# A hybrid decoder step on eight cores: the recurrence's scan writes into another buffer, and every engine's order of work is chosen with new offsets

## The reference, cut to what matters

```python
u = rmsnorm(x, norm_g)
lx, lg, sb, scg, sh, sg, q, qg, mg = jnp.split(u @ w_in, SPLIT_POINTS, axis=-1)
# A: conv(4) -> RG-LRU, SiLU gate path
xc, new_lru_buf = causal_dwconv(lx, lru_buf, lru_conv_w); xc = xc + lru_conv_b
#   r, i = sigmoid(xc @ wa + ba), sigmoid(xc @ wx + bx)      (block diagonal, 6 blocks of 128)
#   log_a = -8 * r * softplus(-lam);  a = exp(log_a)
#   b = sqrt(1 - exp(2*log_a)) * (i * xc);   h_t = a_t * h_(t-1) + b_t
hs, new_h = rglru(xc, lru_h, ...);   z_a = (hs * silu(lg)) @ lru_wo
# B: z_b = (silu(sg) * sb * conv3(scg * sh)) @ sconv_wo
# C: z_c = (softmax(q k' / sqrt(128)) v * silu(qg)) @ xa_wo   (4 heads, 256 memory tokens)
g_a, g_b, g_c = jnp.split(sigmoid(mg), 3, axis=-1)
y = x + (g_a * z_a + g_b * z_b + g_c * z_c) @ w_out          (then a final rmsnorm)
```

## Time and profile before

| | us |
|---|---|
| median of 3 runs (742.28 to 742.45) | 742.34 |
| the profiled execution's own time | 742.75 |
| its span on the slowest core (first to last instruction) | 741.4 |
| spans of the other cores | 738.9 to 740.6 |
| TensorE busy | 704.7 (95%) |
| VectorE busy | 400.1 (54%) |
| ScalarE busy | 345.5 (47%) |
| GpSimd busy | 203.9 (27%) |

### The profile page before, as it was taken

How to read it: one execution, slowest core, us unless ns; L and a number is a source line. 1 busy time by engine, 2 the same in 40 slices (tenths; PEclk the granted TensorE clock), 3 DMA queues, 4 the chain that set the end, 5 groups by cost and what they waited for, 6 DMA issues and landing times.

```text
span 741.4 us, 12905 instructions; the slowest of 8 cores (738.9 to 741.4 us)
## 1 busy us (share of the span) xinstructions
PE 704.7 (95%) x4745; PEld 449.8 (61%) x4745; DVE 400.1 (54%) x391; ACT 345.5 (47%) x457; POOL 203.9 (27%) x268
## 2 busy tenths in 40 slices
PE   1899999999999999999999999999999999999995
PEld 0566666656566566566666666666666666665442
DVE  2455236856459469549784889731323122124666
ACT  3565468585696696894932221212121221213444
POOL 4554001002004002001041436351636363422000
PEclk9999999999999999999999999999999999999998
DMA  8994931112212321222142687853392926038834
GB/s 177 254 242 110 154 67 29 30 30 44 29 29 29 44 29 29 29 34 33 23 82 38 118 172 186 145 80 35 57 138 37 140 35 93 1 118 237 289 147 169
DMA packets 29485, 69.74 MB, mean 94 GB/s; under 512 B 3456, under 2 KB 7872, under 8 KB 29168
## 3 DMA queue, kind: packets, MB, share of 16 engines
q0 software_dynamic: 18000, 31.60, 30.1%
q1 hardware_dynamic: 11424, 37.32, 15.5%
HBM read 90.73 MB, written 9.88 MB: 136 GB/s over the span
## 4 chain that ended last, share of the span: by engine, by line
PE 86%; ACT 4%; DMA 4%; DVE 3%; issue 2%; POOL 0%; SPq 0%; DVEq 0%; ACTq 0%; POOLq 0%
PE PP L649 68%; PE PP L1228 7%; PE PP L692 6%; DMA R<-xp 2%; PE PP L993 2%; ACT R L845 1%; DMA R<-R 1%; PE PP L739 1%; PE PP L923 1%; DMA R<-ck 1%; DVE R L1067 1%; PE PP L985 1%; DVE R L1070 0%; ACT R L727 0%; ACT R L849 0%
## 5 line engine op out<-in xcount | busy, mean ns | idle before, releaser
L649 PE MATMUL PP<-R 128*128 128x344 bf16 x3768 | 558.6, 309 | 7.4 <-ACT R L845 4.3
L649 PEld LDWEIGHTS PP<-R 128*128 128x128 bf16 x3768 | 366.2, 98 | 198.3 <-issue 18.0
L1164 ACT ACTIVATE R<-PP 128x688 f32<-128x688 f32 x72 | 53.5, 743 | 209.5 <-PE PP L649 197.3
L1173 DVE SCALAR_TENSOR_TENSOR R<-R,PP 128x688 f32<-128x688 f32 x72 | 62.1, 868 | 133.1 <-PE PP L649 125.1
L136 POOL DMA_DIRECT2D R<-w_in x68 | 37.6, 553 | 272.1 <-PE PP L649 237.6
L692 PE MATMUL PP<-R 128*128 128x344 bf16 x336 | 53.7, 317 | 3.8 <-DVE R L742 3.2
L1228 PE MATMUL PP<-R 128*128 128x512 bf16 x256 | 55.7, 379 | 0.0
L1177 POOL TENSOR_TENSOR R<-R 128x688 f32<-128x688 f32 x24 | 41.1, 1723 | 45.3 <-DVE R L1173 36.5
L1182 POOL TENSOR_TENSOR R<-R 128x688 bf16<-128x688 f32 x24 | 40.8, 1722 | 20.9 <-DVE R L1173 20.7
L832 DVE SCALAR_TENSOR_TENSOR R<-R 128x2048 f32<-128x2048 f32 x18 | 42.3, 2349 | 7.3 <-ACT R L829 6.2
L692 PEld LDWEIGHTS PP<-R 128*128 128x128 bf16 x336 | 32.8, 100 | 20.2 <-issue 4.4
(11 more groups left out here) (137 smaller groups left out, 572.2 us busy)
## 6 DMA issues: line engine op xcount, KB each, us to landing
R<-w_in POOLq DMA_DIRECT2D x68, 256.0 KB, 4.6
R<-xp SPq DMA_DIRECT2D x32, 512.0 KB, 10.0
R<-ck SPq DMA_DIRECT2D x16, 512.0 KB, 5.1
y_p<-R SPq DMA_DIRECT2D x15, 512.0 KB, 2.6
R<-cv POOLq DMA_DIRECT2D x16, 256.0 KB, 7.8
R<-w_out POOLq DMA_DIRECT2D x8, 256.0 KB, 7.8
R<-xa_wo POOLq DMA_DIRECT2D x14, 128.0 KB, 4.9
R<-lru_wo POOLq DMA_DIRECT2D x8, 192.0 KB, 4.0
```

The costliest lines, as they stand in the source:

```text
L649: return lambda e: e.matmul(ps.ap[:, b * 512:b * 512 + BLK], lhs(k), rhs[:, k, c:c + BLK], start=(k == 0), stop=(k == nk - 1))
L1164: G.act(lambda e, ps=pg[u], th_=th_: e.activation(out=b3(th_.ap), in_=pv(ps), func=AF.Tanh, scale=0.5), UW, [pg[u].tok], [th_.tok], Px - E ...
L1173: G.dve(lambda e, zp=zp, th_=th_, dst=dst: e.scalar_tensor_tensor(out=b3(dst.ap), in0=b3(th_.ap), scalar=1.0, in1=pv(zp), op0=ALU.add, op1 ...
```

## The change: what it does

Four parts.

1. **Scan.** L861, L863, L865 write `a2` in place of `xc`, and L867, L869, L870 read `a2`. The token of `a2` is one for the whole buffer, where `xc` had one for the prompt columns and one for the sample columns. Nothing is added or removed.
2. **Offsets.** Each task gets a key of step and engine (`x2.sp`, `gates3.pe`, `final16.dve`), and a table adds an offset to its priority.
3. **Planner's numbers.** A unit's matmul 0.1465 to 0.1457, a final tile 3.46 to 3.45, the DMA rate at the start 155e3 to 150e3.
4. **Tags** that name the steps.

The table has one entry for nearly every step and engine; of it the lines that the prediction speaks of are shown.

```diff
+SHIFT = {
+    ".dve": -39.5, ".sp": 2.5, "first0.pool": -192.5, "first1.pool": 7, "first2.pool": -16, "x0.sp": -139, "x0.pool": -40.5,
+    "x0.dve": -42, "x0.pe": -6.5, "first3.pool": 11, "x1.sp": -137, "x1.act": 47.5, "x1.pool": -54, "x1.pe": -84.5, "x1.dve": -8,
+    "first4.pool": 47.5, "x2.sp": -349, "x2.act": -2.5, "x2.pool": -7, "x2.dve": 69, "x2.pe": 10.5, "first5.pool": 50, "x3.sp": -107,
+    "x3.pe": -16, "x3.dve": -42.5, "first6.pool": 24, "x4.sp": -40, "x4.act": 0.5, "x4.pool": -15.5, "x4.dve": 2.5, "x4.pe": -60,
+    "first7.pool": 3.5, "x5.sp": -30, "x5.act": 66.5, "x5.pool": -143.5, "x5.pe": 12, "x5.dve": -123, "first8.pool": 8.5, "x6.sp": -29.5,
...
+    "B_sb0.pe": 18.5, "B_sb0.dve": 20, "gates1.pe": 2, "gates1.act": -6, "rec1.act": 31, "rec1.pool": -30, "attend0.pool": 60,
...
+    "A_lx2.act": -2, "conv2.act": -38.5, "conv2.dve": -10.5, "B_sb1.pool": 2, "B_sb1.pe": 2, "B_sb1.dve": 79, "gates2.pe": 2.5,
...
+    "gates3.pe": 11.5, "gates3.act": -31, "rec3.act": -13.5, "rec3.dve": -10.5, "rec3.pool": -6, "attend2.pool": -488, "attend2.pe": -6,
...
+    "conv4.pool": 15.5, "B_sb3.pool": 7.5, "B_sb3.pe": -39, "B_sb3.dve": 0.5, "gates4.pe": -13.5, "gates4.act": 30.5, "rec4.act": -20,
...
+    "sconv5.sp": -56, "scores.sp": -4, "scores.dve": 51.5, "scores.act": -102, "scores.pe": 41.5, "merge00.pe": -41.5, "merge00.act": 7,
...
+    "final14.dve": -23.5, "final14.act": -39, "final15.sp": 53.5, "final15.pe": 108, "final15.dve": 28, "final15.act": 119.5,
+    "final16.sp": 162, "final16.pe": 107.5, "final16.dve": 68.5, "final16.act": 17,
+}
...
+        t.key = f"{self.tag}.{eng}"
+        t.prio += SHIFT.get(t.key, 0.0)
...
-                rate = 155e3 if start < 58.0 else 280e3
+                rate = 150e3 if start < 58.0 else 280e3
...
-            G.pe([mm(k, b) for k in range(nk) for b in range(2)], nk * 2 * 0.1465, reads, [ps.tok], prio, hold)
+            G.pe([mm(k, b) for k in range(nk) for b in range(2)], nk * 2 * 0.1457, reads, [ps.tok], prio, hold)
...
-            G.dve(lambda e: e.tensor_tensor_scan(out=xc[:, 0:T], data0=thr[:, 0:T], data1=thi[:, 0:T], initial=0.0,
-                                                 op0=ALU.mult, op1=ALU.add), T, t_thr + t_thi, [t_xcP], P, mode=0.5)
-            G.dve(lambda e: e.tensor_tensor(out=xc[:, T:TT], in0=thr[:, T:TT], in1=SIT[:, n * 6 + 3, :], op=ALU.mult), TS,
-                  [t_thr[2], m_SIT.t], [t_xcS], P)
...
-            G.dve(lambda e: e.tensor_tensor(out=gA[:, n, :], in0=xc, in1=gA[:, n, :], op=ALU.mult), TT,
-                  [t_xcP, t_xcS] + t_gA[n], t_gA[n], P)
...
+            G.dve(lambda e: e.tensor_tensor_scan(out=a2[:, 0:T], data0=thr[:, 0:T], data1=thi[:, 0:T], initial=0.0,
+                                                 op0=ALU.mult, op1=ALU.add), T, t_thr + t_thi, [m_a2.t], P, mode=0.5)
+            G.dve(lambda e: e.tensor_tensor(out=a2[:, T:TT], in0=thr[:, T:TT], in1=SIT[:, n * 6 + 3, :], op=ALU.mult), TS,
+                  [t_thr[2], m_SIT.t], [m_a2.t], P)
+            G.dve(lambda e: e.tensor_tensor(out=a2[:, T:TT], in0=a2[:, T:TT], in1=thi[:, T:TT], op=ALU.add), TS,
+                  [t_thi[2], m_a2.t], [m_a2.t], P)
+            G.dve(lambda e: e.tensor_tensor(out=gA[:, n, :], in0=a2, in1=gA[:, n, :], op=ALU.mult), TT,
+                  [m_a2.t] + t_gA[n], t_gA[n], P)
+            G.pool(lambda e: e.tensor_copy(SO[:, n, 3:4], a2[:, T - 1:T]), 0.2, [m_a2.t], [t_SO], P + 5)
+            G.pool(lambda e: e.tensor_copy(SO[:, n, 22:38], a2[:, T:TT]), 0.2, [m_a2.t], [t_SO], P + 5)
```

More of the change, by code:

```diff
@@ L212 @@
 class Task:
-    __slots__ = ("i", "eng", "dur", "fns", "reads", "writes", "prio", "hs", "tset", "npred", "succ", "pf", "dma", "preds", "start", "gate", "etset", "xgate", "stores")
+    __slots__ = ("i", "eng", "dur", "fns", "reads", "writes", "prio", "hs", "tset", "npred", "succ", "pf", "dma", "preds", "start", "gate", "etset", "xgate", "stores", "key")
+SHIFT = {
[47 rows of a table added]
+    "sconv5.sp": -56, "scores.sp": -4, "scores.dve": 51.5, "scores.act": -102, "scores.pe": 41.5, "merge00.pe": -41.5, "merge00.act": 7,
[24 rows of a table added]
+}
 EXP = frozenset((0, 6))
@@ L229, in __init__ @@
         self.touch = {}
+        self.tag = ""
     def _shared(self, k):
@@ L724, in p0 @@
         def p0(ti, src, nr, dst, gcols, tdst, prio, wait):
+            G.tag = f"x{ti}"
             x_, xn_, ps = Handle(xring), Handle(xnring), Handle(PS, 1)
@@ L752, in build_program @@
             while len(w_toks) < len(first) and len(w_toks) < i + LEAD:
+                G.tag = f"first{len(w_toks)}"
                 hw, lhs = wload(w_in_cols(first[len(w_toks)]), -200 + i)
@@ L764, in build_program @@
             p0(17 + i, memp[i * 128:(i + 1) * 128, :], 128, mnT[:, :, i * 128:(i + 1) * 128], pT[:, 8:16], t_mn[i], -80 + i, w_toks[-1:])
+        G.tag = "states"
         for k in ("sin", "out"):
@@ L827, in branch_A_lx @@
                 G.act(lambda e, p=p: e.copy(out=p.dst(lxp, 3), in_=p.src()), p.n, [p.tok], [t_lx[p.u]], P - EV + p.u, psum=True)
+            G.tag = f"conv{n}"
             cw = lambda k: pT[:, 16 + k * 6 + n:17 + k * 6 + n]
@@ L848, in branch_A_gates @@
             P = P - 4 - AB
+            G.tag = f"rec{n}"
             G.act(lambda e: e.activation(out=a2, in_=thr, func=AF.Exp, scale=dv[:, 6 + n:7 + n], bias=dv[:, 6 + n:7 + n]), TT,
@@ L887, in branch_B_c @@
             P += 7.02
+            G.tag = f"sh{n}"
             for u, ps in enumerate(proj(C_SH + n * 128, P)):
@@ L890, in branch_B_c @@
                       [ps.tok, t_sc[u]], [t_ci[u]], P - EV + u)
+            G.tag = f"sconv{n}"
             sw = lambda k: pT[:, 64 + k * 6 + n:65 + k * 6 + n]
@@ L962, in heads_q @@
             P += 8
+            G.tag = "qs"
             tq = m_tq.ap.rearrange("p (c b h) -> p c b h", c=2, h=4)
@@ L980, in attend @@
                 P1 = P + tb * 8.55
+                G.tag = f"att{hd}{tb}"
                 ps, ps2, pe_, rd_ = Handle(PS), Handle(PS), Handle(pering), Handle(rdring)
@@ L1011, in step @@
             nonlocal pos
+            G.tag = f.__name__.replace("branch_", "") + str(a[0])
             f(*a, pos)
@@ L1019, in build_program @@
         step(branch_A_lx, 0)
+        G.tag = "kv"
         kv(pos + KVP)
@@ L1025, in build_program @@
             if n < NCH:
+                G.tag = f"gates{n}"
                 branch_A_gates(n, pos + 10.73)
@@ L1151, in build_program @@
             if j == 0:
+                G.tag = "scores"
                 sample_scores(P, 8.0)
             if j == 4:
+                G.tag = "values"
                 sample_values(P - 5, 2.5)
@@ L1158, in build_program @@
                 Px = P + xi * 12
+                G.tag = f"merge{j}{x}"
                 ths = [Handle(thring) for _ in range(NU)]
@@ L1185, in build_program @@
             if j == NJS:
+                G.tag = "fix"
                 fix_samples(P + 6)
@@ L1237, in whole_tile @@
             tile_in(ti, x_)
-            G.pe([f for b in range(2) for f in tile_mm(ti, b, lambda b=b: ps.ap[:, b * 512:(b + 1) * 512])], 3.46,
+            G.pe([f for b in range(2) for f in tile_mm(ti, b, lambda b=b: ps.ap[:, b * 512:(b + 1) * 512])], 3.45,
                  tile_reads(ti * 128, ti * 128 + 128), [ps.tok], P)
@@ L1312, in build_program @@
             P = PF + i * 3.5
+            G.tag = f"final{i}"
             if ti == 16:
```

4 lines of the change are left out of this document (removed), and 60 rows, old and new, of the table SHIFT.

## The result

The changed kernel takes 747.35 us (median of 4 runs, 746.13 to 749.7) against 742.31 (742.17 to 742.45): ratio 1.007, 95% interval 1.0049 to 1.0091. It is slower by 0.7%, and 2.9 us above the top of the range.

What follows compares the result with a forecast made beforehand. TensorE bounds the kernel, busy 704.7 of 741.4 us, leaving 36.7 idle. Start -0.6, gates -2.7, scan 0, merge 0, end -0.7 and new waits +1.0 make -3.0: 739.3 on the median, own range 736.5 to 741.5, full range 734.5 to 744.5.

Steps and rivals of the forecast that it cites:

- New waits: Anywhere in the new order: one misfit between estimated and real durations, +1.0 us, ends 0 and +5.0.
- the score copy: Merge: VectorE waits 8.76 us for the 32 KB copy, priced by the planner at 3.2; TensorE lost 1.4.
- Start: Before the first projections: late `par` costs +0.5, tile 5 is 1.0 us earlier; -0.6 in all, ends -3.0 and +1.0.
- Gates and front: TensorE's waits for ScalarE to empty PSUM, 5.4 us: half removed, -2.7, ends -5.4 and +1.0.
- Scan: Six scans: earlier free `xc` saves only ScalarE time that TensorE's work hides; 0, ends -0.8 and +0.3.
- Merge: VectorE's wait before L1076 for the score copy comes later; 0, ends -1.4 and +5.0.
- End: Behind the last matmul: L1250 goes first and the last store has 256 KB; -0.7 us, ends -1.1 and +0.5.
- the gates' waits under 3 us: Sign for the front: TensorE's waits for L845 under 3 us in all, against 4.3.
- the second block's wait under 1 us: Sign for the start: the wait before 33.31, for tile 5's L742, falls from 1.75 to under 1 us.
- The first piece at 21.3 to 21.7: Sign for the start: first projection piece at that time after three L742 back to back, against 21.04 before.
- a busy time of TensorE within 1 us: Sign for the whole kernel: busy time, 704.7 us before, stays the same; a larger move means wrong reasons.
- The third rival: Merge, score copy uncovered: +5.0 us, giving 744.3, or 746.5 if the clock falls too; chance 0.16.

Runs made afterwards that it cites:

- run 1: Changed kernel with one weight load of the fourth block's branch A put ahead of the six small GpSimd copies: 741.39 us, ratio 0.9986 to the kernel before.
- run 2: Changed kernel with that weight load ahead of the copies and two merge weight loads ahead of GpSimd's waiting sums: 737.50 us, ratio 0.9933 to the kernel before.
- run 7: Kernel before with one front weight load, issued 60 us ahead of its use, put behind the load near 239 us: 749.72 us, ratio 1.0097.
- run 10: Changed kernel with three loads earlier, three products ahead of the last tiles' transposes, and the start in the old order: 734.55 us, ratio 0.9898 to before.
- run 5: Kernel before, its order kept, with only the scan's edit (scan in `a2`, L863's small product moved behind L861): 742.49 us, ratio 1.0002.
- run 4: Changed kernel with the three weight loads earlier and `par` with its small operations first: 739.69 us, ratio 0.9959 to the kernel before.
- run 11: Changed kernel, same offsets, planner's price of GpSimd's six small copies raised from 0.2 to 2.3 us, planned anew: 760.22 us, ratio 1.0248 to the kernel before.
- run 8: Kernel before with one front weight load made late and eight small GpSimd fills ahead of it: 751.06 us, ratio 1.0115.
- run 3: Changed kernel with the parameter DMA `par` first on SP and the small operations on it first, weight loads untouched: 746.73 us, ratio 1.0065 to before.

## Why the prediction was wrong

**The failed step is "New waits", taken as +1.0 with an upper end of +5.0.** On the slowest core of the profiled execution it was 9.0 of waits for weights and 4.5 of clock behind two of them, 13.5; at the median, 2.35 lower, some 11 (an estimate from these two times). The step argued from the one misfit it had seen, the score copy, and asked of no other producer how early it is. The DMAs that GpSimd issues were priced nowhere in the sum but at the start, though the change moves nearly all of them. The trace of before held the warning: copies of 2.2 us beside equal ones of 0.2, right ahead of a weight load. Runs 1, 2 and 7 show the mechanism, by removal and by making it.

**The metric was left out too.** The forecast was made for one core. The waits differ by core (2.4 to 9.0 us of `w_in`), and the time is the worst of eight. Core 4 ended at 734.7, 6.7 under the slowest core before; core 1 at 748.3. The average core, at most 1.1 us above before, missed the forecast of -3.0 by 3 to 4; the rest of the miss, which is 8.0 by the medians, is the spread between cores, for which the sum had no term.

**The sum without the new waits came out near, and in part by luck.** It was -4.0. With the late loads removed (run 2) the kernel is 5.0 us under before by the ratio. But the front gained almost three times its forecast, and losses for which no term stood took the difference away.

- *Start*, -0.6: wrong in sign. The first piece came 3.2 late, not 0.5. `par` did land behind the tiles (VectorE waits for it until 18.21), as forecast. But the step missed three things: ScalarE's first table load, which before was done at 3.06 with the operations on `par`, now stands ahead of the first square (8.44, 1.28 us); the tile used third was scaled behind the two products that wait for `par` (20.48), and a fourth tile's transposes stood ahead of the first piece. Part of it was made up, since TensorE had no wait of over 0.4 between 24 and 68 us, where before there were 1.8, 0.6, 0.3 and 0.3. Against that stand new ones of 0.57, 0.23 and 1.70 at 68 to 74 us. Averaged over the cores, TensorE waited 2.1 us more before 92 us than in the kernel before. Run 10, which puts the old order of the start back, gained 0.8 to 1.3 us.
- *Gates and front*, -2.7: far too small. 17 waits, 5.4 in all, became two or three, 0.4 to 0.7 in all (run 2 and the changed kernel, but for the weights). The step took half because it could not follow the order, and it priced a wait at its idle time alone. Before, on core 6:

```profile
152.04 0.45 PE L649 MATMUL PP<-R 128*128 128x344 bf16 x2 [0.27 <-ACT R L845]
152.84 0.45 PE L649 MATMUL PP<-R 128*128 128x344 bf16 x2 [0.35 <-ACT R L845]
```

  Two matmuls at full pace take 0.29, but the row with the wait of 0.35 starts 0.80 behind the one before it: each wait costs 0.16 more than it shows. With 15 waits gone that makes about -7.4, past the -5.4 that the prediction took for its end. It also lowers TensorE's busy time: 701.4 on core 4, where the slowest core before had 704.7. Against that stand some 1.8 us of clock in 60 to 80 us (20 us at 0.91) on five of eight cores, which no step had.
- *Scan*, 0: right, by run 5.
- *Merge*, 0: half right. Before, only three cores waited there (1.4, 0.9 and 0.2). In the changed kernel the copy had landed by the time VectorE came to it on core 1, and on the others VectorE waited 0.4 to 4.7 us for it, but TensorE did not. Once the late loads were gone it showed as 1.0 to 2.5 us on some cores (runs 2 and 4), far from +5.0.
- *End*, -0.7: the order came as forecast, L1344's halves ahead of L1388 and L1396, but it brought only -0.2 over the eight cores (-0.5 on core 4, +0.5 on core 1).

Of the signs named beforehand, the gates' waits under 3 us (0.3), the second block's wait under 1 us (0.3) and the halves ahead of the last tile's scale came. The first piece at 21.3 to 21.7, the first table load at 17 or later (8.44) and a busy time of TensorE within 1 us (706.8 on core 1, 701.4 on core 4, against 704.7) did not. The last was named as the sign of a forecast that rests on the wrong reasons, and it was one: the low clock added busy time on the slow cores, and the saved waits took some away on all.

**The third rival was right in kind and wrong in place.** An engine's list was held up by a misjudged operation, TensorE ran out of work, and the clock fell. It did so behind GpSimd's copies and sums and not behind the score copy. The forecast gave that case a surcharge of 2.2 us for the clock after 6 us of idleness; it came after 3.8 us already, twice, as 1.8 and 2.7. The page "TensorE: Matmul & The Clock Gate" of the Trainium skill, section "HAM oscillation — how this bites in real kernels", says that gaps bring the lower clock back; run 7 agrees, with 0.52 after a wait of 5.33 us and 3.0 us lost.

What stays open: why core 3 kept its clock after a wait of 3.4 us at 190 and core 6 lost a part of it after 3.2 (the three cores that kept it there, 3, 4 and 7, are those that also kept it at 60 to 80 us), and what makes the landing of equal loads differ between cores and executions by 2 us.

## What to carry to other kernels

When a change re-sorts a whole schedule, first list every load by how long before its first use it goes out, and look at what stands ahead of it on the engine that issues it: a load that depends on nothing belongs ahead of small operations and of sums that wait for others. Price a wait of a full TensorE as its length plus the slower stretch behind it, and by the worst core, not the mean. A plan made from wrong prices can spend the slack that hid them; mending one price afterwards makes a new plan (run 11), while moving three loads by hand in the found plan kept its gains.

## What the runs showed of the hardware that was not expected

- A GpSimd copy of 128x1 to 128x16 in fp32 took 0.2 us, and 2.1 to 2.3 beside a VectorE operation with two inputs of 128x2048 or 128x2064 fp32 in SBUF: it ended when that one ended.
- After a wait of 3.8 us within dense work the granted clock of 5 us was 0.50, and matmuls took 0.26 us each in place of 0.146. At 68 to 74 us three waits of 0.57, 0.23 and 1.70, close together, went with a clock of 0.91 over 20 us on five of eight cores (six in run 2), and with a full one on the others.
- The price of a late load has a step: in run 7 2.7 to 3.2 us of clock came on top of waits of 3.7 to 5.3, and in run 8, with waits of 6.3 to 6.6, it was 1.8 to 2.5. In the traces of the changed kernel and of runs 1 and 3 every wait of 3.5 to 4.4 us cost 1.8 to 2.8 more behind it; of fifteen waits of 2.6 to 3.4 us seven cost 1.5 to 3.0 more and eight nothing.
- An interruption of dense matmuls costs more than its idle time: units of two matmuls between waits came 0.16 us later each than the idle time and the pace of 0.146 give.
